# Turning finished heads into another PSUM bank, and later in the output projection

## The reference, cut to what matters

```python
def probs(qb, k):
    sc = einsum("bqhd,bkhd->bhqk", qb, k) * scale
    return softmax(where(causal, sc, NEG_INF))
w = probs(qb1, k1) - lam * probs(qb2, k2)          # differential attention
diff_out = einsum("bhqk,bkhd->bqhd", w, v)
...
log_stick = cumsum(log_one_minus, reverse=True) - log_one_minus
a = where(strict, exp(log_beta + log_stick), 0.0)  # stick-breaking attention
sb_out = einsum("bhqk,bkhd->bqhd", a, v)
...
mixed = concatenate([rmsnorm(diff_out) * (1.0 - lam_init), rmsnorm(sb_out)])
x = x + mixed @ w_out
h = rmsnorm(x)
x = x + square(relu(h @ w_mlp_in)) @ w_mlp_out
```

## Time and profile before

| | us |
|---|---|
| median of 3 runs | 2146.78 (2145.99, 2146.78, 2147.34) |
| the profiled execution, its own time | 2147.38 |
| its span in the trace | 2145.6 |
| PE busy | 2063.8 |
| DVE busy | 1285.7 |
| ACT busy | 969.4 |
| POOL busy | 66.6 |

### The profile page before, as it was taken

One profiled execution on the slowest core, in us unless ns is written; L12 is line 12 of the kernel. 1 busy time (PEld: TensorE's weight loads), 2 busy tenths in 40 slices (PEclk: granted clock), 3 DMA queues, 4 the chain that ended last, 5 costly groups with the idle time before them and its releaser, 6 DMA issues.

```text
span 2145.6 us, 32731 instructions
## 1 busy us (share of the span) xinstructions
PE 2063.8 (96%) x12774; PEld 1807.3 (84%) x12774; DVE 1285.7 (60%) x1746; ACT 969.4 (45%) x1397; POOL 66.6 (3%) x78
## 2 busy tenths in 40 slices
PE   8999999999999999888999999899999999999997
PEld 7898798988888898768889887788888888888886
DVE  6798765466565666566555655566555555655654
ACT  5554444344444444334345545544434434434443
POOL 2000021000000000000000000100000000000000
PEclk9999999999999999998999999999999999999999
DMA  8334576645454545553545544455566566556552
GB/s 270 99 109 169 170 216 206 171 132 170 135 166 137 166 138 162 199 171 109 166 125 161 158 119 156 166 181 183 198 194 187 192 192 189 183 200 192 187 196 89
DMA packets 199537, 359.86 MB, mean 168 GB/s; under 512 B 21488, under 2 KB 30000, under 8 KB 198768
## 3 DMA queue, kind: packets, MB, share of 16 engines
q1 hardware_dynamic: 197616, 352.01, 52.7%
q0 software_dynamic: 1600, 5.96, 0.9%
q10 hardware_dynamic: 192, 0.05, 0.0%
HBM read 355.88 MB, written 2.10 MB: 167 GB/s over the span
## 4 chain that ended last, share of the span: by engine, by line
PE 53%; issue 38%; DVE 6%; ACT 2%; POOL 0%; DMA 0%; ACTq 0%; DVEq 0%; POOLq 0%
PE acc L484 23%; PE acc L488 19%; PE acc L566 1%; DVE w_low L1645 1%; ACT w_high L1068 1%; PE banks L812 1%; PE banks L898 1%; PE banks L841 1%; PE banks L767 1%; PE banks L629 1%; PE banks L827 0%; PE banks L917 0%; PE banks L550 0%; PE banks L901 0%; PE banks L836 0%
## 5 line engine op out<-in xcount | busy, mean ns | idle before, releaser
L1645 DVE TENSOR_TENSOR w_low<-raw,w_high 128x1024 fp32r<-128x1024 f32 x648 | 792.6, 1229 | 677.3 <-ACT w_high L1068 675.7
L1068 ACT ACTIVATE w_high<-raw 128x1024 fp32r<-128x1024 f32 x648 | 683.2, 1059 | 775.5 <-PE acc L484 341.9
L488 PE MATMUL acc<-x_high_low,w_high 128*128 128x256 f32 x2432 | 359.4, 287 | 2.0 <-issue 2.0
L484 PE MATMUL acc<-w_high,x_high_low 128*128 128x512 f32 x1152 | 323.9, 394 | 3.9 <-ACT transposed_tmp L1453 3.9
L488 PEld LDWEIGHTS acc<-x_high_low,w_high 128*128 128x128 f32 x2432 | 321.2, 194 | 4.2 <-issue 3.0
L484 PEld LDWEIGHTS acc<-w_high,x_high_low 128*128 128x128 f32 x1152 | 211.6, 188 | 47.2 <-issue 3.7
L488 PE MATMUL acc<-x_high_low,w_low 128*128 128x256 f32 x1216 | 196.7, 284 | 0.0
L484 PE MATMUL acc<-w_high,h_high 128*128 128x512 f32 x560 | 175.7, 395 | 6.3 <-DVE w_low L1645 3.7
L484 PE MATMUL acc<-w_low,x_high_low 128*128 128x512 f32 x576 | 178.3, 391 | 0.0
L484 PE MATMUL acc<-w_low,h_high 128*128 128x512 f32 x560 | 173.8, 392 | 0.0
L484 PE MATMUL acc<-w_high,h_low 128*128 128x512 f32 x560 | 173.6, 391 | 0.0
(11 more groups left out here) (358 smaller groups left out, 2157.7 us busy)
## 6 DMA issues: line engine op xcount, KB each, us to landing
raw<-in_b_w_in SPq DMA_DIRECT2D x128, 512.0 KB, 3.7
raw<-in_w_mlp_in SPq DMA_DIRECT2D x128, 512.0 KB, 3.7
raw<-in_w_mlp_out SPq DMA_DIRECT2D x128, 512.0 KB, 3.6
raw<-in_w_in SPq DMA_DIRECT2D x96, 512.0 KB, 4.1
raw<-in_kv_w SPq DMA_DIRECT2D x48, 512.0 KB, 4.3
raw<-in_a_w_in SPq DMA_DIRECT2D x32, 512.0 KB, 4.9
raw<-in_b_w_out SPq DMA_DIRECT2D x32, 512.0 KB, 4.2
raw<-in_w_out SPq DMA_DIRECT2D x32, 512.0 KB, 3.6
```

What stands on the lines that cost most here:

```text
L484: ins_ = nc.tensor.matmul(PAIRS[pair][:, t, :], xa[:, kt + j, t * P:(t + 1) * P], wa[:, k, j, :], start=first and n == 0, stop=last and n ...
L488: ins_ = nc.tensor.matmul(ACC[pair][:, m // 2, (m % 2) * TOK:(m % 2 + 1) * TOK], wa[:, k, j, m * P:(m + 1) * P], xa[:, kt + j, :], start=f ...
L1068: nc.scalar.activation(WH[:, s % SPLIT, :, :], RAW[:, s, :, :], ACT.Copy).then_inc(hi_ready, SLOTS + 1 if first_one else 1)
L1645: V.tensor_tensor(WL[:, k, :, :], RAW[:, p % SLOTS, :, :], WH[:, k, :, :].bitcast(F32), ALU.subtract).then_inc(lo_ready, SLOTS + 1 if isin ...
```

## The change

Three things are different. `head_turn` of a differential head writes bank 3 in place of bank 2, and the wait for the copy of the head before moves from `diff_turn` and `head_turn` to `weigh`. `head_turn` and `head_copy` of the second stick-breaking half come at `i = 4 * h + 11` in place of `4 * h + 9`, and its `head_split` at `4 * h + 12` in place of `4 * h + 10`; that is one tick later in the output projection. The last split then falls behind the thirteenth tick of DVE, which is written out.

```diff
         def diff_turn(n):
             pe.wait_ge(w_dve, n + 1)
-            pe.wait_ge(tr_tmp, TR_MIX + 8 * (n // 4) + n % 4)
+            if n % 4 == 0:
+                pe.wait_ge(tr_tmp, TR_MIX + 8 * (n // 4))
+            else:
+                pe.wait_ge(b_act, n)
...
             if order:
                 pe.wait_ge(on_dve, order)
+            if 1 <= order % 8 <= 4:
+                pe.wait_ge(tr_tmp, TR_MIX + order)
...
         def head_turn(order, turned):
             pe.wait_ge(on_dve, order + 1)
-            pe.wait_ge(b_act, turned)
-            if order:
+            bank = BK[3] if order % 8 < 4 else BK[2]
+            if order % 8 >= 4:
+                pe.wait_ge(b_act, turned)
                 pe.wait_ge(tr_tmp, TR_MIX + order)
             for t in range(NT):
-                ins_ = nc.tensor.transpose(BK[2][:, t * P:(t + 1) * P], ON[:, order % 2, t, :], ID)
+                ins_ = nc.tensor.transpose(bank[:, t * P:(t + 1) * P], ON[:, order % 2, t, :], ID)
...
-                    if i == 4 * h + 9:
+                    if i == 4 * h + (11 if j else 9):
                         head_turn(order, 4 * j + 4)
...
-            nc.scalar.activation(TMP[:, order % 2, 0, :], BK[2][:, 0:TOK], ACT.Identity, bias=0.0,
+            nc.scalar.activation(TMP[:, order % 2, 0, :], BK[2 if kind else 3][:, 0:TOK], ACT.Identity, bias=0.0,
...
-                    if i == 4 * h + 9:
+                    if i == 4 * h + (11 if j else 9):
                         head_copy(1, order)
...
-                    if i == 4 * h + 10:
+                    if i == 4 * h + (12 if j else 10):
                         head_split(order, 8 + 4 * j + h)
...
-        for c, ticks in enumerate((4, 0, 8, 8)):
+        low(0)
+        second_stage("sb", 1, 24)
+        for c, ticks in enumerate((3, 0, 8, 8)):
             low(0, ticks)
```

## The result

The changed kernel takes **2151.91 us** (median of 11 runs, 2148.43 to 2154.47), against 2146.78 of the kernel before (11 runs, 2144.17 to 2147.87): 5.1 us more, ratio 1.0023 with an interval of [1.0014, 1.0033]. It is slower where 2142.0 was forecast, and outside the range. The profiled execution took 2152.38 with a span of 2150.6.

What follows compares the result with a forecast made beforehand. PE was taken to bound the kernel, with DVE's chain limiting the gain in the projection. Differential heads 1.76 plus projection 3.3 gave 5.1 us off the profiled 2147.38, or 2142.3; 2142.0 was put for the median, range 2138.8 to 2145.0.

Steps and rivals of the forecast that it cites:

- What stalls later is untouched.: Behind the output projection: stalls stay as before, so no gain or loss was counted there.
- No instruction is added: Differential heads: turning into bank 3 with the moved wait adds no instruction and moves no DMA on either queue.
- slower: Rival: ACT's copy comes after the product with the values, PE stands at seven or eight products; 2152 us, chance 0.03.
- Differential heads, 1.76 us: Differential attention: 0.17 us saved at each of five heads, 0.91 at n = 1, of 5.5 us stall.
- about 0.8 at a differential head: Differential heads: cost of each half clock stretch at a new head, the wait for the probabilities covering the rest.
- The moved wait costs nothing: Differential heads, at `weigh`: the copy ends 3.4 us before the product starts, so PE does not wait.
- DVE's chain bounds the projection: Output projection: DVE's 9.74 us period limits PE; the later split shortens it by 0.05 to 0.61 a head, taken as 0.33.
- The last product 3.23 us earlier: Output projection, `weigh` of head 3: starts at 1355.27 instead of 1358.50, of which 1.38 and 0.20 are the clock's.
- From there to tick 13, 10.2: Output projection, last product to tick 13: 10.2 us, same as before, with a new wait of about 0.9 for the split.
- The projection saves 3.3, of which 1.6 the clock: Output projection: total saving 3.3 us (3.23 + 0.05), about 1.6 of it from avoiding half clock.
- half clock again: Rival, projection: PE's wait at the last product costs 1.58 again, 2143.6 to 2144.2; chance 0.38 shared with POOL held.

Runs made afterwards that it cites:

- The bank alone: Changed kernel with turn, copy and split back at their old ticks and 8 instructions added ahead of the MLP loop: 2144.08 us, ratio 0.999 against the kernel before.

## Why the prediction was wrong

The step that failed is a sentence at the end of the projection, **"What stalls later is untouched."** I looked for what a moved step does to the buffers and engines behind it, and found nothing, rightly. But "No instruction is added" was itself the trap: eight are taken away, and in a program with a loop behind them that moves the loop's start against the blocks in which PE gets its instructions. That cost 7.87 us in the profiled execution. None of my rivals had it; "slower" had 0.03, on a mechanism (the moved wait) that did not act. With the loop's start elsewhere the same steps gave 2143.07 (8 instructions) and 2141.92 (136), near the forecast of 2142.0. That nearness is in part luck: in the profiled execution of the first the heads gave nothing in place of 1.76, the projection 3.57, and its time is 2144.16 where the sum gives 2142.3.

- **Differential heads, 1.76 us: oversized.** The wait for the probabilities came in place of the copy's, as told: at n = 2 the time from the head's scores to L911 is 1097.39 - 1090.58 = 6.81, against 1097.77 - 1090.80 = 6.97, so 0.16 less where 0.17 was worked out, with 0.50 idle for `probs_first`. But the stage took 261.68 against 261.62. TensorE fell to half clock at two places where it had not before. Windows of the changed kernel (busy, PEclk, DMA share, GB/s):

```profile
1110.00:1120.00 10.00, 10.00 (x73) 0.83 0.25 70
...
1275.00:1300.00 25.00, 25.00 (x156) 0.93 0.44 139
```

  and of the kernel before:

```profile
1110.00:1120.00 10.00, 9.35 (x76) 1.00 0.28 79
...
1275.00:1300.00 25.00, 24.34 (x159) 1.00 0.45 148
```

  The prediction had a price for this, "about 0.8 at a differential head". From L911 of head 2 to L911 of head 3 it takes 1114.80 - 1097.39 = 17.41 with such a stretch between, where it took 16.70 before and 0.17 less was expected. That makes 0.9 each, and two of them are the whole 1.76. The bank alone fell at two new places too (from 1090.3 and from 1107.4) but not at n = 1, where the kernel before had fallen, and saved 0.74. The kernel with 232 instructions more fell once in the heads and saved 2.04. The mechanism was right; the term took the clock of one trace as given, while the condition was named and left out of the sum.
- **The moved wait costs nothing: right.** No wait for the copy stands at the products of the differential heads.
- **DVE's chain bounds the projection: right, the share per head undersized.** I took 0.33 a head between 0.05 and 0.61. DVE and POOL in the changed kernel:

```profile
1339.20 0.56 DVE L2393 TENSOR_TENSOR stick_b<-stick_b,stick_a 128x384 f32<-128x384 f32 x1 [2.43 <-ACT stick_a L1555]
...
1341.97 1.22 DVE L1651 TENSOR_TENSOR w_low<-raw,w_high 128x1024 fp32r<-128x1024 f32 x1
1342.10 1.65 POOL L2585 TENSOR_TENSOR head_small<-head_small,minus_half 128x2 f32<-128x2 f32 x1 [5.02 <-DVE head_small L2331]
...
1343.43 0.42 DVE L1679 TENSOR_TENSOR h_low<-transposed_tmp,h_high 128x256 fp32r<-128x256 f32 x1
1343.78 0.61 DVE L2336 TENSOR_SCALAR head_rows<-banks,head_small 128x128 f32<-128x128 f32 x2
...
1348.33 0.56 DVE L2393 TENSOR_TENSOR stick_b<-stick_b,stick_a 128x384 f32<-128x384 f32 x1 [2.43 <-ACT stick_a L1555]
```

  The period is 1348.33 - 1339.20 = 9.13 against 9.74, so 0.61, the upper bound. POOL ended at 1343.75, before the split's second instruction did (1343.43 + 0.42 = 1343.85), and DVE's scaling no longer waits. The Trainium skill (GPSIMD Engine Reference, Specifications) says that GpSimd contends with DVE instructions that have two SBUF inputs; by it alone POOL would have been held behind L1679 too. Here the measurement decides: POOL ended 0.56 after `low`, as it had ended 0.54 after it before, and got through beside the split. That `low` holds it is borne out by the last head of the kernel before, where the same instruction ran without a `low` beside it (1360.47) and took 0.69 in place of 1.59.
- **The last product 3.23 us earlier: 3.82.** From the first scores of the projection it comes at 1355.39 - 1317.76 = 37.63, against 1358.50 - 1317.05 = 41.45. With 0.61 in place of 0.33 the step's own sum gives 3.79. PE's waits for the mask were 0.80, 0.84 and 1.52, where I had about 1.0, 1.5 and 2.1, and the small one for `stick_c` did not come.
- **From there to tick 13, 10.2: right.** 1365.68 - 1355.39 = 10.29, with the new wait for the last split at 0.67 of idle, in starts the 0.9.
- **The projection saves 3.3, of which 1.6 the clock: right in kind, 3.6.** Tick 16 comes 3.58 earlier, and the clock alone gave 1.57 in the run with the old ticks.
- **The rival "half clock again" in the projection did not come.** PEclk was 1.00 there in the changed kernel and in each of the runs that carry a part of it.

A version that beats both kernels is the changed one with its loop away from the boundary: 2143.07 with 8 instructions in front of the loop, 3.7 us or 0.17% under the kernel before, and 2141.92 with 136 (0.20%), which differ by less than their runs do.

## What to carry to other kernels

In a program with a loop, any edit that adds or takes away instructions on an engine ahead of the loop, be it a wait, can move the time by more than what the edit is for: here 8 instructions of 32731 made 7.9 us, twice the gain. So compare "issue" waits at the jumps back before a small difference is put down to the steps that were edited, and try the loop's start at another distance before a change is judged. The harmless places are wide (no stall at 8, 136 and 208 instructions, half a microsecond at 232), so one pad tells, if it is more than a few instructions: 4 and 6 made the stall longer.

## What the runs showed that I had not expected

- Where PE stopped behind a jump back, it went on 3.4 to 5.8 us after the end of its last weight load ahead of the jump (1776.38 to 1780.32 and 1958.52 to 1961.94 in the changed kernel, 1960.47 to 1966.31 with 256 instructions more). Work that lies between the jump's target and the block's end is done in that time for free.
- In the changed kernel half clock followed the stop of 2.53 us and not that of 2.00. In the kernel before with 8 instructions fewer it followed the second stop, of 3.10 (PEclk 0.94 from 1948 to 1975), and not the first, which was 2.53 again (PEclk 1.00 from 1774 to 1800). So the length of the stop alone does not settle it.
- Which differential heads fall to half clock changed between kernels that do the same there: n = 1, 3 and 7 in the changed kernel (from 1076.3, 1110.4 and 1281.1), n = 2 and 3 with the bank alone (from 1090.3 and 1107.4), only n = 7 with 232 instructions more (from 1277.8). What decides it stays open, and it moves the heads' time by up to 2 us.
